# Scaled keys by block level, one convolution channel block on TensorE, one product per forgetting score, and clock-holding products taken out

## The reference

```python
u = val * jax.nn.sigmoid(gate)          # convolution: y[t,c] = sum over 31 taps of w[tap,c] * u[t-30+tap,c]
...
log_a = jax.nn.log_sigmoid((glr @ gate_w2 + gate_b).astype(f32)) / GLA_GATE_TAU
...
b = jnp.cumsum(gi, axis=2)
diff = b[:, :, :, None, :] - b[:, :, None, :, :]
decay = jnp.exp(jnp.where(causal[:, :, None], diff, -jnp.inf))
attn = jnp.einsum('bhtk,bhsk,bhtsk->bhts', qi, ki, decay)
```

```python
logits = jnp.einsum('bhqd,bhkd->bhqk', q[:, :, lo:hi], k[:, :, :hi]).astype(f32) * scale
logits = logits + c[:, :, lo:hi, None] - c[:, :, None, :hi]
```

## Time and profile before

| | |
|---|---|
| three timed runs, median (lowest, highest) | 4144.97 us (4140.25, 4145.49) |
| the profiled execution, its own time | 4149.23 us |
| its span, first to last instruction | 4147.1 us |
| mean granted TensorE clock | 0.944 |
| TensorE busy | 3840.6 us (93%) |
| VectorE busy | 3010.4 us (73%) |

### The profile page before, as it was taken

The page is one execution under the profiler, slowest core; times in us unless marked ns, Lnnn a source line. Parts: engine busy times, 40 slices in busy tenths (PEclk is TensorE's granted clock), DMA queues, the critical chain, the costliest instruction groups (busy, mean ns, idle before and its releaser), DMA issues. The chain is left out here.

```text
span 4147.1 us, 72340 instructions
## 1 busy us (share of the span) xinstructions
PE 3840.6 (93%) x29271; PEld 3471.3 (84%) x29271; DVE 3010.4 (73%) x5918; ACT 1798.7 (43%) x3638; POOL 337.3 (8%) x243
## 2 busy tenths in 40 slices
PE   6998999997899679999999997998999999998698
PEld 6996899996798569899998885798899988897597
DVE  7776778785677677987677854589776787787665
ACT  3444545443443424434444452444444444544343
POOL 0000000000000004830000000067200000000000
PEclk9999999997799869999999996899999999999699
DMA  8766476763266314434444442243444444675243
GB/s 317 274 243 227 188 264 239 264 249 132 82 259 233 132 41 163 153 133 166 171 167 170 163 176 88 88 168 142 144 173 168 168 163 173 234 298 210 92 173 142
DMA packets 118990, 749.74 MB, mean 181 GB/s; under 512 B 13185, under 2 KB 13345, under 8 KB 43265
## 3 DMA queue, kind: packets, MB, share of 16 engines
q1 hardware_dynamic: 117650, 740.97, 48.2%
q10 hardware_dynamic: 688, 3.11, 0.2%
q0 software_dynamic: 320, 1.05, 0.1%
HBM read 742.98 MB, written 1.05 MB: 179 GB/s over the span
## 5 line engine op out<-in xcount | busy, mean ns | idle before, releaser
L931 ACT ACTIVATE weights_high<-weight_ring 128x512 fp32r<-128x512 f32 x2248 | 1294.8, 624 | 1225.7 <-PE bank L194 908.5
L939 DVE TENSOR_TENSOR weights_low<-weight_ring,weights_high 128x512 fp32r<-128x512 f32 x2016 | 1299.3, 689 | 608.6 <-ACT weights_high L931 603.7
L194 PE MATMUL bank<-h_high,weights_high 128*128 128x256 f32 x4800 | 1369.6, 285 | 29.3 <-POOL weights_low L939 10.3
L194 PE MATMUL bank<-h_low,weights_high 128*128 128x256 f32 x4800 | 1362.5, 284 | 0.0
L194 PE MATMUL bank<-h_high,weights_low 128*128 128x256 f32 x4800 | 1362.1, 284 | 0.0
L194 PEld LDWEIGHTS bank<-h_high,weights_high 128*128 128x128 f32 x4800 | 924.5, 193 | 44.8 <-issue 20.9
L194 PEld LDWEIGHTS bank<-h_low,weights_high 128*128 128x128 f32 x4800 | 924.8, 193 | 9.0 <-issue 0.2
L194 PEld LDWEIGHTS bank<-h_high,weights_low 128*128 128x128 f32 x4800 | 924.6, 193 | 0.0
L194 PE MATMUL acc<-weights_high,hidden_high 128*128 128x512 f32 x1552 | 613.3, 395 | 0.0
L194 PE MATMUL acc<-weights_low,hidden_high 128*128 128x512 f32 x1552 | 606.4, 391 | 0.0
L194 PE MATMUL acc<-weights_high,hidden_low 128*128 128x512 f32 x1552 | 604.2, 389 | 0.0
(11 more groups left out here) (283 smaller groups left out, 3561.7 us busy)
## 6 DMA issues: line engine op xcount, KB each, us to landing
weight_ring<-stream SPq DMA_DIRECT2D x581, 1024.0 KB, 4.8
h_tok<-slots SPq DMA_DIRECT2D x100, 512.0 KB, 5.7
h_feat<-slots SPq DMA_DIRECT2D x90, 512.0 KB, 6.0
work<-slots SPq DMA_DIRECT2D x26, 512.0 KB, 8.4
mod_sums<-biases SPq DMA_DIRECT2D x7, 1536.0 KB
h_feat<-rows SPq DMA_DIRECT2D x8, 512.0 KB, 3.7
work<-biases SPq DMA_DIRECT2D x1, 1536.0 KB
x_tok<-x ACTq DMA_DIRECT2D x1, 1024.0 KB, 5.5
```

What stands on the lines that cost most here:

```text
L194: ins = self.nc.tensor.matmul(out, lhs, rhs, start=start, stop=stop)
L931: act.activation(k.w_hi[:, b, q * self.QUARTER:(q + 1) * self.QUARTER], self.raw(g, q), ACT.Copy).then_inc(k.highs_ready, 1)
L939: return eng.tensor_tensor(k.w_lo[:, b, w], self.raw(g, q), k.w_hi[:, b, w].bitcast(F32), ALU.subtract)
```

## The change

There are five parts. First, `hold_clock` goes from the boundaries with sums altogether, and from between the transposes at the others: 118 of 169 dummy products. Second, VectorE does the taps of three channel blocks. For the fourth, ScalarE makes 31 diagonal matrices 128x128 (14 ahead of the log-sigmoid, 17 behind it), and TensorE does 31 float32 products 128x128 by 128x256 into `acc`: 2 behind the low-rank product, 8 behind z, 21 in `GlaScale`. With three operations to a tap instead of four, VectorE does 2, 3 and 3 taps in `GlaDecays` (6, 9 and 9 operations), 3 per head in `GlaAttend` (9 operations) and the last 5 at its end (15). Third, the keys are scaled by levels: near blocks of 32 keys for each 16 queries, and three levels of pairs of blocks of 32, 64 and 128 tokens, each with one border. That is 3072 columns in two groups of 1536 instead of 6656. A head's products become 16 of 32 keys by 16 queries, 4 of 32x32, 2 of 64x64 and 1 of 128x128, written at partition offsets. ScalarE zeroes four banks for them. Fourth, the fox scores carry -c as one more row of the key tile with a row of ones in the queries: even heads have 65 rows, odd heads a whole 128-row tile with zeros between. `HeadNorm` gets four fills on ScalarE, `ToHeads` copies each bank in two halves, GpSimd issues 16 DMAs that put the 16 rows of -c in place, and `Scores` waits for them. The slot with the head-picking matrix goes. Fifth, arguments follow.

```diff
@@ -547,8 +549,6 @@
         if self.sums is not None:
             pe.wait_ge(k.mod_used, self.sums.done)
             for j in range(2 * DC):
-                if j % 4 == 0:
-                    self.hold_clock(k.bank[:, 2, :], 2)
                 mm = k.mm(self.column_sums()[:, j:j + 1], self.sums.where[:, j * P:(j + 1) * P],
                           k.small[:, ONES:ONES + 1], start=True, stop=True, last=True)
             mm.then_inc(k.banks_for_vector.sem, k.banks_for_vector.send())
@@ -559,13 +559,12 @@
                 mm = pe.transpose(self.turned(c, t), self.source(t)[:, c * P:(c + 1) * P], k.c("ident"))
                 if c % 4 == 3:
                     mm.then_inc(k.feature_banks.sem, 1)
-            if t == 0:
-                self.hold_clock(k.bank[:, 2, :], 2)
         if self.sums is not None and not self.gate_later:
             for h in range(2):
                 mm = self.gate_row(pe, h)
             mm.then_inc(k.banks_for_scalar.sem, k.banks_for_scalar.send())
-        self.hold_clock(k.acc[:, 2, :], 4)
+        if self.sums is None:
+            self.hold_clock(k.acc[:, 2, :], 4)
...
@@ -1946,22 +1945,19 @@
 
     def tensor(self, pe):
         k = self.k
-        if self.extra:
-            pe.wait_ge(k.slot_landed[(self.s) % RING], k.loads(self.s))
+        if self.decays:
+            pe.wait_ge(k.decays_landed, 16 * self.decays)
...
             def product(bank, t=t, h=h, n=n):
-                mm = k.mm(bank, q(h)[:, t * P:(t + 1) * P], kt(h)[:, 0:n], start=True,
-                          stop=product_extra is None, last=True)
-                return mm if product_extra is None else product_extra(bank, t, h, n)
+                return k.mm(bank, q(h)[:, t * P:(t + 1) * P], kt(h)[:, 0:n], start=True, stop=True, last=True)
...
+class ToHeads(ToFeatures):
+
...
+    def evacuate(self, eng, parity):
+        k = self.k
+        taken, sent = (k.banks_for_vector, k.vector_for_tensor) if parity == 0 else (k.banks_for_scalar, k.scalar_for_tensor)
+        for i, (t, c, n) in enumerate(self.steps):
+            if i % 2 != parity:
+                continue
+            eng.wait_ge(taken.sem, taken.take())
+            src = k.bank[:, i % NB, 0:n * P].rearrange("p (c q) -> p c q", q=P)
+            even = self.dst[0:HD, c:c + n, t * P:(t + 1) * P]
+            odd = self.odd[c // DC][HD:P, c % DC:c % DC + n, t * P:(t + 1) * P]
+            for dst, half in ((even, src[0:HD]), (odd, src[HD:P])):
+                ins = eng.tensor_copy(dst, half) if parity == 0 else eng.activation(dst, half, ACT.Copy)
+            ins.then_inc(sent.sem, sent.send())
+
+    def gpsimd(self, pool):
+        k = self.k
+        for h in range(FOX_HEADS):
+            key = self.dst[HD:HD + 1, DC + h // 2, :] if h % 2 == 0 else self.odd[1][0:1, h // 2, :]
+            pool.dma_start(key, self.decays[h:h + 1, :]).then_inc(k.decays_landed, 16)
...
     def scalar(self, act):
-        take_root(self.k, act, self.k.small[:, 16:16 + TT * self.n])
+        k = self.k
+        finite = lambda n: k.c("ident")[0:n].unsqueeze(1).to_broadcast([n, TT * DC, P])
+        for tile in self.odd:
+            act.activation(tile[0:HD].rearrange("p c (t q) -> p (c t) q", q=P), finite(HD), ACT.Copy,
+                           scale=0.0).then_inc(k.act_step, 1)
+            done = k.step("act")
+        act.wait_ge(k.act_step, done)
+        one = k.small[:, ONES:ONES + 1]
+        act.activation(self.odd[0][0:1].rearrange("p c (t q) -> p (c t) q", q=P), finite(1), ACT.Identity, scale=0.0,
+                       bias=one[0:1])
...
+        take_root(k, act, k.small[:, 16:16 + TT * self.n])
...
-        dve.tensor_copy(self.c_t, k.bank[0:H, 1, 0:S])
+        dve.tensor_scalar(self.c_t, k.bank[0:H, 1, 0:S], -1.0, None, ALU.mult)
...
-        k, n = self.k, CONV // P
+        k, n = self.k, CONV // P - 1
         for tap in range(self.at, end):
...
+    def make_diagonals(self, act, end):
+        k, last = self.k, (CONV // P - 1) * TAPS
+        for tap in range(self.made, end):
+            act.activation(self.diagonals[:, tap, :], k.c("ident"), ACT.Identity,
+                           scale=self.w[:, last + tap:last + tap + 1]).then_inc(k.diagonals, 1)
+        self.made = end
+
+    def products(self, pe, end):
+        k, c = self.k, CONV // P - 1
+        for tap in range(self.product, end):
+            pe.wait_ge(k.diagonals, tap + 1)
+            mm = k.mm(k.acc[:, 2, 0:S], self.diagonals[:, tap, :], self.u[:, c, tap:tap + S], start=tap == 0,
+                      stop=tap == TAPS - 1, last=True)
+        self.product = end
+        if end == TAPS:
+            mm.then_inc(k.banks_for_scalar.sem, k.banks_for_scalar.send())
+
+    def take_products(self, act):
+        k, c = self.k, CONV // P - 1
+        act.wait_ge(k.banks_for_scalar.sem, k.banks_for_scalar.take())
+        act.activation(self.y[:, c, :], k.acc[:, 2, 0:S], ACT.Identity, bias=self.b[:, c:c + 1])
...
+        self.convolve.products(pe, 2)
...
+        self.convolve.products(pe, 10)
...
+        self.convolve.make_diagonals(act, 14)
         log_sigmoid(self.k, act, self.z, self.tmp)
+        self.convolve.make_diagonals(act, TAPS)
...
-        self.convolve.taps(dve, taps + 4)
+        self.convolve.taps(dve, taps + 5)
...
-        self.convolve.taps(dve, taps + 6)
+        self.convolve.taps(dve, taps + 8)
...
+    def tensor(self, pe):
+        self.convolve.products(pe, TAPS)
 
     def scalar(self, act):
         k = self.k
...
+        near, far = self.scaled.near, self.scaled.far
+        for part in (near, far):
+            act.wait_ge(k.vector_for_scalar.sem, k.vector_for_scalar.take())
+            act.activation(part, part, ACT.Exp).then_inc(k.scalar_for_vector.sem, k.scalar_for_vector.send())
+        for h in range(GLA_HEADS):
+            act.activation(k.bank[:, h, :].rearrange("p (a b) -> p a b", b=P),
+                           k.c("ident").unsqueeze(1).to_broadcast([P, 4, P]), ACT.Copy, scale=0.0)
+        self.convolve.take_products(act)
 
     def vector(self, dve):
-        k = self.k
+        k, at, b = self.k, self.scaled, self.b_t
         dve.memset(self.ref[:, :, 0:1], 0.0)
-        dve.tensor_copy(self.ref[:, :, 1:N_SUB], self.b_t[:, :, SUB - 1:S - 1:SUB]).then_inc(k.dve_step, 1)
+        dve.tensor_copy(self.ref[:, :, 1:N_SUB], b[:, :, SUB - 1:S - 1:SUB]).then_inc(k.dve_step, 1)
         dve.wait_ge(k.dve_step, k.step("dve"))
...
+        ref = self.ref.rearrange("p a n -> p (a n)")
+        cut = lambda v, n: v.rearrange("p a (m i) -> p (a m) i", i=n)
+        dve.tensor_tensor(at.q, cut(b, SUB), ref.unsqueeze(2).to_broadcast([P, 2 * N_SUB, SUB]), ALU.subtract)
+        blocks = [P, S // SUB, 2, 2 * SUB]
+        own = lambda v: cut(v, 2 * SUB).unsqueeze(2).to_broadcast(blocks)
+        dve.tensor_tensor(at.keys, ref.rearrange("p (m two) -> p m two", two=2).unsqueeze(3).to_broadcast(blocks),
+                          own(b), ALU.subtract).then_inc(k.dve_step, 1)
+        dve.wait_ge(k.dve_step, k.step("dve"))
+        keys = at.keys.rearrange("p m two i -> p (m two i)")
+        dve.tensor_scalar(keys, keys, CLAMP, None, ALU.min).then_inc(k.vector_for_scalar.sem, k.vector_for_scalar.send())
+        for n, q, key in at.levels:
+            both = cut(b, 2 * n)
+            border = both[:, :, n - 1:n].to_broadcast([P, S // n, n])
+            dve.tensor_tensor(q, both[:, :, n:], border, ALU.subtract)
+            ins = dve.tensor_tensor(key, border, both[:, :, 0:n], ALU.subtract)
+        ins.then_inc(k.vector_for_scalar.sem, k.vector_for_scalar.send())
         dve.wait_ge(k.scalar_for_vector.sem, k.scalar_for_vector.take())
...
+        dve.scalar_tensor_tensor(at.q, cut(self.q_t, SUB), HD ** -0.5, at.q, ALU.mult, ALU.mult)
+        dve.tensor_tensor(at.keys, at.keys, own(self.k_t), ALU.mult)
+        dve.wait_ge(k.scalar_for_vector.sem, k.scalar_for_vector.take())
+        for n, q, key in at.levels:
+            dve.scalar_tensor_tensor(q, cut(self.q_t, 2 * n)[:, :, n:], HD ** -0.5, q, ALU.mult, ALU.mult)
+            dve.tensor_tensor(key, key, cut(self.k_t, 2 * n)[:, :, 0:n], ALU.mult)
...
+class Scaled:
+
+
+    def __init__(self, buffer):
+        self.near, self.far = buffer[:, 0:6 * S], buffer[:, 6 * S:12 * S]
+        self.q = self.near[:, 0:2 * S].rearrange("p (a i) -> p a i", i=SUB)
+        self.keys = self.near[:, 2 * S:].rearrange("p (m two i) -> p m two i", two=2, i=2 * SUB)
+        part = lambda i, n: self.far[:, i * S:(i + 1) * S].rearrange("p (a i) -> p a i", i=n)
+        self.levels = [(n, part(2 * j, n), part(2 * j + 1, n)) for j, n in enumerate((32, 64, 128))]
+
+    def blocks(self, hp):
+        out = [(b // 2 * 2 * SUB, 2 * SUB, self.keys[:, hp * (N_SUB // 2) + b // 2, b % 2, :], b * SUB, SUB,
+                self.q[:, hp * N_SUB + b, :]) for b in range(N_SUB)]
+        for n, q, key in self.levels:
+            out += [(2 * n * m, n, key[:, hp * (S // (2 * n)) + m, :], 2 * n * m + n, n,
```

(20 more changed lines are left out.)

100 lines of the change are left out of this document (34 added, 66 removed).

## The result

The changed kernel took 4069.02 us (median of three, 4067.28 to 4075.93) against 4144.97: ratio 0.9824, 95% interval 0.9802 to 0.9847. So the change is worth 76 to 83 us where 60 were forecast. The profiled execution took 4067.28 us, its span 4065.5.

The account below looks back on a forecast made before the run. The prediction took waits between TensorE (93% busy) and VectorE (73%) as what a gain could come from. Terms -11.5, +1.6, -7.3, -11.5 and -31, with 1 for the stream, made -60: 4085 us from 4145, 8-in-10 range 4062 to 4110.

Parts of the forecast that it names:

- case D: `GlaAttend` and fox scores: small products packed by the array, scores at VectorE's pace; -9 and -4 more, 4072 us, chance 0.15.
- Boundaries with sums: -11.5 forecast: Eight boundaries: waits for sums go, -15.5; end dummies, -3; transposes, +2; weight products at the lower clock, +5.
- The term of +5: Eight boundaries with sums: first weight products run at the lower clock; half of a possible +10.8 us was charged.
- Boundaries without sums: 0 forecast: Three boundaries: two dummy products between transposes go, the clock is 1.00 there and 13 in front stay; counted 0.
- `GlaDecays`: +1.6 forecast: Two diagonal products ahead of z cost 1.3 us (the first term), VectorE's extra operation 0.3 past the present wait.
- `GlaScale`: -7.3 forecast: Key scaling: 11.5 us for what took 18.8, fewer columns on VectorE, 21 diagonal products on TensorE; ends -9 and +1.7.
- `GlaAttend`: -11.5 forecast: Head steps 6.4 us for 9.4, -9; first head, -3.6; end taps, +1.2; small products at 0.25 us; ends 0 and -20.
- Fox scores: -36 forecast: Fox mixer: 32 score jobs take 24 us instead of 60.2, between 30 at the old product price and VectorE's pace.
- DMAs of GpSimd: +5.5 forecast: Fox mixer: 16 DMAs issued at 0.62 us, 2.5 us to land, delay the scores; ends +3.5 and +17.
- Rival A: Eight weight stages: without dummies the clock stays at the lower level for long; 4150 us or more, chance 0.03.
- B: `GlaAttend` gains about 0, small products keeping their price; `GlaScale` loses 1.7, diagonal products at lower clock; 4105 us, chance 0.17.
- C: Fox mixer: GpSimd's DMAs land late, +17 instead of +5.5, or products keep their price; 4091 to 4103 us, chance 0.15.

Follow-up runs that it names:

- e1: The kernel before the change with only the 118 dummy products taken out: 4131.06 us, ratio 0.9963.
- e2: The changed kernel with two dummy products put back between the transposes of each of the three boundaries without sums: 4063.85 us, ratio 0.9801.
- e12: The same edit to the changed kernel as e2, run once more beside the others: 4068.23 us, ratio 0.9809.
- e3: The changed kernel with the convolution's fourth channel block back on VectorE, no diagonal products, keys by levels kept: 4079.27 us, ratio 0.9843.
- e7: The changed kernel with each head's near key blocks reordered so that four neighbours share a partition offset: 4061.93 us, one execution.
- e6: The changed kernel with each head's near key blocks reordered so that neighbours never share a partition offset: 4070.51 us, one execution.
- e10: The changed kernel with the middle dummies back and the 16 rows of -c moved by two DMAs instead of 16: 4059.93 us, ratio 0.9798.
- e9: The changed kernel with the middle dummies back and 13 taps of the third channel block moved to TensorE in `GlaAttend`: median 4073.2 us, ratio 0.9812.
- e11: The changed kernel with the middle dummies back, 13 taps on TensorE and two DMAs for -c, all together: 4061.97 us, ratio 0.9789.

## Why the prediction was right or wrong

The sign, the places and the order of size were right, and 4069 lies in the range. The sum was 16 us short, since what came was nearer to case D of the prediction (4072, chance 0.15) than to the forecast. The parts below are read from one pair of executions 82 us apart, so they add up to 22 us short.

- **Boundaries with sums: -11.5 forecast, -19.7 between the traces, -18.2 by e1.** The waits went as worked out (16.6 to 1.3 us), though the 16 sums took 4.5 us and not 3.3, 1.7 of it at the lower clock. The term of +5 for weight stages that begin at the lower clock failed. I took it from the output projection of the even mixer, behind 17 us of idle TensorE. At a boundary the lower clock came early and was over by the time the weights began. That is so at all eight after the change: the dip ended 0.8 to 2.9 us ahead of the first weight product (one of them has a second dip 8 us into the weights, as it had before the change). In the boundary of rows 3 the clock was 0.50 in the earlier trace rows, and after the change it was up again at the first weight product, which starts at 1141.5. The windows there, after:

```profile
1134.00:1139.00 5.00, 4.23 (x19) 3.75 (x20) 4.40 (x15) 3.96 (x10) 0.00 (x0) 0.50 0.00 0
1140.00:1142.00 2.00, 1.76 (x8) 0.72 (x7) 1.97 (x5) 1.97 (x5) 0.00 (x0) 1.00 0.00 0
```

- **Boundaries without sums: 0 forecast.** This was wrong. With two dummy products between the transposes the clock never fell there, and without them it fell at two of three. I took the clock of 1.00 in the earlier trace rows as needing nothing. The boundary of that row did keep it in the changed kernel, but I had looked at one of three, and the other two lost it. Up to `ForgetGates` the fox stretch is 1.7 us longer; the cost in the whole time stays open (e2, e12).
- **`GlaDecays`: +1.6 forecast, +0.3 measured** (18.3 us from its first tap to `GlaScale` before, 18.6 after). The size of the first term was wrong, not the price of a product. The two products ahead of z took 1.13 us, near the 0.9 of the forecast, but they began while VectorE was still copying the low-rank result (until 1421.56), so z came only 0.5 us later. The extra tap went into a wait, which fell from 0.71 to 0.21 us. The clock gave nothing here: the cumulative sum took 3.68 us for 3.78, at the lower level for most of it.

```profile
1421.04 1.13 PE L196 MATMUL acc<-work 128*128 128x256 f32 x4
1422.10 1.13 PE L196 MATMUL bank<-work 16*128 16x256 f32 x4
...
1429.81 3.68 PE L196 MATMUL bank<-constants,work 128*128 128x256 f32 x8 [2.92 <-DVE work L2516]
```

- **`GlaScale`: -7.3 forecast, -9.2 measured.** The clock was 1.00 throughout, so the 21 products took 9.34 us, the lower end of my range.
- **`GlaAttend`: -11.5 forecast, -21.6 measured.** This is the term that was mis-sized most. I took 0.25 us for a small product, a guess between its old price and VectorE's limit. It was 0.076, so VectorE decided and not TensorE. e3 shows that the clock isn't the reason, and e7 that column groups add some; the rest is left for the narrow key block. The rule of the Trainium skill, "TensorE: Matmul & The Clock Gate", Part 3, that small products in distinct column groups run concurrently, was my rival D. e7 (8.93 for 6.98 us) agrees with it, e6 (6.87) shows no more to be had by it. It pointed at the right end, but more for another reason: in e7, with most of that overlap gone, VectorE still decided.
- **Fox scores: -36 forecast, -39.7 measured** (60.7 us to 21.1), at VectorE's pace. Products of 65 and 128 rows took 0.43 us each at the lower clock, not 0.72: alternating 64 and 16 rows had been dearer than full height. **DMAs of GpSimd: +5.5 forecast, +2.4 measured.** They issued at 0.48, not 0.62, and landed in 2.0 us. e10 takes 1.8 of that back. With the 1.7 us of the dip and 1.3 us more behind the scores, for which no cause is shown, this gives the fox mixer's -34.3.
- **No part of the diff**: -1.2 us up to the first boundary, and +3.9 in the expert parts, which hold one of the dips just named (1.7 us of it by the price above). Other dips of the clock in unchanged stages moved from execution to execution.

Rival A (the clock stays low in weight stages) is refuted by e1. B (small products keep their price, diagonal products run at the lower level) and C (the DMAs land late, or the fox products keep their price) are refuted by the rows of the changed kernel itself: 0.076 us, 9.34 us for 21 products, 2.0 us to land and 0.43 us. D's times came in both halves (-10 and -4 more than forecast), though packing is only a part of the first.

## What to carry to other kernels

Don't price a small product by the instruction: look at the columns it loads and at where its neighbours write. A quarter of the width gave a quarter of the time (0.40 to 0.094 us at the lower clock), overlap of pairs included. Two edits in one stage are not additive: moving work off an engine is worth nothing until the engine that ends last has been made faster, so try them together as well as alone. Dummy work that keeps a clock up must be tested place by place: at eight boundaries it cost 18 us and kept nothing, at three others two dummies each kept the clock up in 18 cases of 18, where without them it fell in 15 of 24.

## What was not expected of the hardware

A float32 product of 64 rows by 32 columns by 16 took 0.036 us among neighbours in other column groups (2.3 us for 64) and 0.069 among its own (4.4). Thirteen diagonal products in the middle of `GlaAttend` lifted that stage's clock from 0.63 to 0.91, in e9 and again in e11. The window in e9:

```profile
1442.00:1461.00 19.00, 16.68 (x242) 14.17 (x236) 18.01 (x48) 4.99 (x15) 0.00 (x0) 0.91 0.01 1
```

And the scatter between executions of one kernel, 20 us in 4060, goes with the mean granted clock (0.957 at 4053.8 us, 0.949 at 4082.2 us in e9).
